# One step of a hybrid GLA/Fourier backbone: the first stage in an order by token blocks

## The reference

```python
mod = silu(cond) @ w_ada + b_ada                  # shift, scale, gate: 6 x 1024
h   = rmsnorm(x + pos, g_pre_mix) * (1 + sc_m) + sh_m
z   = h @ w_in        # [q | k | v | g | lowrank_fwd | lowrank_bwd | u]
la  = log_sigmoid(lowrank @ w_a2 + b_a2) / 16     # decays of the linear attention
o   = rmsnorm(gla(q, k, v, la, both directions), g_head) * silu(g)
y   = concat(o, real(fft2(u))) @ w_out
x   = x + gt_m * rmsnorm(y, g_post_mix)
x   = x + gt_f * rmsnorm(relu(h2 @ w_fc1)**2 @ w_fc2, g_post_mlp)
```

## Time and profile before

| | |
|---|---|
| median of three runs | 1338.31 us |
| the profiled execution's own time | 1342.97 us |
| its span, first to last instruction | 1341.2 us |
| PE busy | 1250.0 us (93%) |
| DVE, ACT, POOL busy | 774.5, 425.7, 129.7 us |
| mean granted clock of TensorE | 0.961 |
| moved by the DMA engines | 97.24 MB |

### The profile page before, as it was taken

How to read it: one execution, slowest core, us unless ns; L and a number is a source line. 1 busy time by engine, 2 the same in 40 slices (tenths; PEclk the granted TensorE clock), 3 DMA queues, 4 the chain that set the end, 5 groups by cost and what they waited for, 6 DMA issues and landing times.

```text
span 1341.2 us, 18877 instructions
## 1 busy us (share of the span) xinstructions
PE 1250.0 (93%) x7421; PEld 742.2 (55%) x7421; DVE 774.5 (58%) x1253; ACT 425.7 (32%) x736; POOL 129.7 (10%) x258
## 2 busy tenths in 40 slices
PE   2779999999896798989999999999999999999997
...
DMA packets 70894, 97.24 MB, mean 73 GB/s; under 512 B 3093, under 2 KB 53402, under 8 KB 70810
## 3 DMA queue, kind: packets, MB, share of 16 engines
...
## 4 chain that ended last, share of the span: by engine, by line
PE 55%; DVE 1%; ACT 0%; issue 0%; POOL 0%; POOLq 0%; ACTq 0%; DVEq 0%
PE bank L1221 55%; DVE region L2060 0%; DVE ghb L2060 0%; ACT bank L886 0%; ACT whi L615 0%; DVE region L2173 0%; DVE region L2175 0%; POOL small L797 0%; DVE region L2049 0%; ACT region L1137 0%; ACT region L1142 0%; DVE region L2186 0%; DVE region L2075 0%; POOL small L795 0%; POOLq L289 0%
## 5 line engine op out<-in xcount | busy, mean ns | idle before, releaser
L1221 PE MATMUL bank<-whi,region 128*128 128x512 f16 (+1 forms) x1872 | 491.4, 348 | 5.9 <-ACT region L1117 4.5
L1221 PE MATMUL bank<-region,whi 128*128 128x384 f16 (+1 forms) x1872 | 459.4, 328 | 11.0 <-DVE wlo L627 11.0
L1221 PE MATMUL bank<-wlo,region 128*128 128x512 f16 (+1 forms) x936 | 326.1, 348 | 0.0
L1221 PE MATMUL bank<-region,wlo 128*128 128x384 f16 (+1 forms) x936 | 307.3, 328 | 0.0
L1221 PEld LDWEIGHTS bank<-whi,region 128*128 128x128 f16 x1872 | 184.3, 98 | 166.2 <-issue 9.2
L1221 PEld LDWEIGHTS bank<-region,whi 128*128 128x128 f16 (+1 forms) x1872 | 183.5, 98 | 133.5 <-DVE wlo L627 11.3
L2141 DVE SCALAR_TENSOR_TENSOR region<-bank,small,region 128x512 f32<-128x512 f32 x126 | 93.2, 749 | 158.8 <-PE bank L1221 158.4
L615 ACT ACTIVATE whi<-stage,small 128x2048 f16<-128x2048 f32 (+1 forms) x42 | 82.3, 1959 | 300.6 <-PE bank L1221 294.2
L1221 PE MATMUL bank<-region 128*128 128x512 f16 (+8 forms) x802 | 160.6, 372 | 17.2 <-DVE small L1611 5.4
L2123 DVE TENSOR_TENSOR region<-region 128x384 f32<-128x384 f32 x96 | 53.5, 557 | 182.0 <-ACT region L1189 182.0
L1221 PEld LDWEIGHTS bank<-region 128*128 128x128 f16 (+4 forms) x802 | 102.0, 164 | 66.5 <-issue 13.5
...
## 6 DMA issues: line engine op xcount, KB each, us to landing
...
region<-in_x_sample SPq DMA_DIRECT2D x8, 512.0 KB, 10.8
...
```

The costliest lines, as they stand in the source:

```text
L1221: return nc.tensor.matmul(out, lhsT, rhs, start=start, stop=stop, skip_group_check=True)
```

## The change

The first stage is written out step by step for each engine.

- **Loads.** The first ada chunk comes first, then the small vectors, then tiles and chunks in turn: all ada chunks and the chunks LR and Q are loaded with x0 to x3, and x4 to x8 behind them. Six rooms hold the ada chunks in place of eight.
- **Positions.** The row half of the embedding is no longer loaded 64-fold: 16 rows are loaded, and PE multiplies them by a selection (`spread_pos`, eight f32 matmuls of 16 rows, 128 x 512). DVE copies each to `posr` (`put_pos`) and adds it (`add_pos`); the column half is added by POOL (`add_col`).
- **Blocks.** Before the gains, only x0 to x3 are turned. x4 and x5 are turned behind the first products of block 0, x6 to x8 between those of block 1. PE's order from the gains on: LR and the first Q tile of block 0, x4, x5, the second Q tile, the spread of K's maximum; LR and Q of block 1 with x6 and x7 between, K's tiles of blocks 0 and 1 with x8 between; LR and Q of block 2, the logits, K of block 2. The copies from PSUM and the high and low parts on ACT and DVE follow this order.
- **Low rank.** `low_rank_tile` puts the eight inner slices into four column groups of the array (24 matmuls with 32 columns as before, six in each group); the four partial sums stay apart on 128 partitions, and w_a2, loaded four times, adds them in the logits (128 rows in place of 32).
- **Decays.** `logits(0)` comes behind the last product of Q and behind four of K's six. From the product U_A on the order is that of before.

```diff
-    start = []
-    for what in "x0 a0 x1 a1 x2 x3 a2 x4 a3 x5 x6 a4 x7 x8 a5 a6 a7".split():
...
-    for what, n in start:
+    start = [("rows", 0), ("pos", 1), ("pos", 2), ("rows", 1), ("out", 0), ("x", 0), ("pos", 3), ("rows", 2), ("out", 1),
...
+    first = [("z", LR, 0, 0), ("z", Q, 0, 0), ("x", 4), ("x", 5), ("z", Q, 1, 0), ("sc", K),
...
-        ada_room = [R1[:, 2048 * i:2048 * i + 2048] for i in range(4)] + [R34[:, 2048 * i:2048 * i + 2048] for i in range(4)]
-        xh = [R1[:, 8192:9216], R34[:, 8192:9216]]
+        ada_room = [R1[:, 2048 * i:2048 * i + 2048] for i in range(4)] + [R34[:, 2048 * i:2048 * i + 2048] for i in range(2)]
+        xh = [R34[:, 7168:8192], R34[:, 8192:9216]]
+        lr_pair = [R34[:, 6400 + 128 * x:6528 + 128 * x].bitcast(F16) for x in range(2)]
...
+        wa2 = R34[:, 4608:4608 + 512]
+        lrS = R34[:, 5120:5120 + TOK]
+        row16 = gex[0:16].rearrange("p b n -> p (b n)")
+        row_sel = whi[1][0:16, :].bitcast(F32)
...
+            load_ada(0)
+            sp.dma_start(consts[:, 0:C_MASK], a["k_consts"][:, 0:C_MASK]).then_inc(s_const, 16)
...
-                    sp.dma_start(posr[64 * r:64 * r + 64, j - 1:j + 1],
-                                 pos_rows[r, j - 1:j + 1].partition_broadcast(64)).then_inc(s_pos[j // 2], 16)
...
+            sp.dma_start(row16, a["k_pos_row"]).then_inc(s_prow, 16)
+            sp.dma_start(posc, a["k_pos_col"]).then_inc(s_pcol, 16)
+            load_x(0)
+            load_ada(1)
...
+            sp.wait_ge(s_wa2, 1)
+            for q in range(4):
+                for d in range(2):
+                    r = 2 * RANK * q + RANK * d
+                    sp.dma_start(wa2[r:r + RANK, 256 * d:256 * d + 256], a["w_a2"][0, d]).then_inc(s_misc, 16)
...
-            for j in range(NT):
+            def add_col(j):
...
+                nc.gpsimd.tensor_tensor(x1[:, j, 512:D], x1[:, j, 512:D], posc, ALU.add).then_inc(s_posc, 1)
+            nc.gpsimd.memset(wa2, 0.0).then_inc(s_wa2, 1)
+            x_rstd(0)
+            add_col(1)
+            x_rstd(1)
+            add_col(2)
...
+            x_rstd(3)
+            add_col(4)
+            add_col(5)
+            add_col(6)
+            x_rstd(4)
+            x_rstd(5)
...
-            for what, n in start:
-                if what == "x":
-                    if n + 2 < NT:
-                        square_x(n + 2)
-                    if n + 1 < NT:
-                        norm_x(n + 1)
-                elif what == "rows":
-                    mod_part(n, ada1[n])
...
+            chunk_high(act, LR)
+            mod_part(5, ada1[5])
+            square_x(3)
+            norm_x(3)
+            mod_part(6, ada1[6])
+            chunk_high(act, Q)
+            mod_part(7, ada1[7])
             act.wait_ge(s_gn, 1)
...
+            def put_first(key):
+                _, i, m, t = key
+                bank = take_z(key)
+                dst = lrS if i == LR else (qT, kT)[i - Q][:, m, :]
+                nc.scalar.activation(dst[:, TBW * t:TBW * t + TBW], bank[:, 0:TBW], ACT.Copy,
...
+            high_x(0, 0)
+            high_x(0, 1)
+            square_x(4)
+            square_x(5)
+            norm_x(4)
+            norm_x(5)
+            put_first(("z", LR, 0, 0))
+            high_x(1, 0)
+            put_first(("z", Q, 0, 0))
...
+            chunk_high(act, K)
+            square_x(6)
+            square_x(7)
+            norm_x(6)
...
+            put_first(("z", Q, 0, 2))
+            put_first(("z", Q, 1, 2))
+            chunk_high(act, U_A)
+            decay_logs(0)
+            put_first(("z", K, 0, 2))
+            put_first(("z", K, 1, 2))
...
+            def spread_pos(j):
+                if j == 1:
+                    pe.wait_ge(s_prow, 16)
+                    pe.wait_ge(s_psel, 1)
+                bank = A.open(pe, ("pos", j))
+                mm(bank[:], row_sel[:, P * (j - 1):P * j], row16, True, True).then_inc(A.filled(("pos", j)), 1)
...
-            for i in range(G_A):
+            def low_rank_tile(key):
+                t = key[3]
+                wh, wl = pair(LR)
+                bank = A.open(pe, key)
+                toks = slice(TBW * t, TBW * t + TBW)
+                pe.wait_ge(s_tl, 2 * t + 2)
+                for kk in range(2):
+                    for n, (w, x) in enumerate(((wh, HTh), (wh, HTl), (wl, HTh))):
+                        for q in range(4):
+                            r = 2 * RANK * q
+                            ins = nc.tensor.matmul(bank[r:r + 2 * RANK, 0:TBW], w[:, 2 * q + kk, :], x[:, 2 * q + kk, toks],
+                                                   start=kk == 0 and n == 0, stop=kk == 1 and n == 2,
+                                                   tile_position=(0, r), skip_group_check=True)
+                ins.then_inc(A.filled(key), 1)
...
+                else:
+                    if step_[3] == 0 and step_[2] == 0:
+                        pe.wait_ge(s_wlo, n + 1)
+                    if n == LR:
+                        low_rank_tile(step_)
+                    else:
+                        up_tile(step_, 0, n, step_[2], step_[3], HTh, HTl).then_inc(A.filled(step_), 1)
...
-                if i == Q:
-                    logits(0)
...
             def add_pos(j):
                 dve.wait_ge(s_x[j], 16)
-                dve.wait_ge(s_pos[(j - 1) // 2], 48 if j <= 2 else 32)
-                own.did(V.tensor_tensor(x1[:, j, 0:512], x1[:, j, 0:512], posr[:, j - 1, :], ALU.add))
-                V.tensor_tensor(x1[:, j, 512:D], x1[:, j, 512:D], posc, ALU.add).then_inc(s_posd, 1)
+                A.wait_read(dve, ("pos", j))
+                V.tensor_tensor(x1[:, j, 0:512], x1[:, j, 0:512], posr[:, j - 1, :], ALU.add).then_inc(s_posd, 1)
...
+            dve.wait_ge(s_const, 16)
+            V.tensor_copy(row_sel.rearrange("p (r t) -> p r t", t=64),
+                          ident[0:16, 0:16].unsqueeze(2).to_broadcast([16, 16, 64])).then_inc(s_psel, 1)
+            def put_pos(j):
+                bank = A.take(dve, ("pos", j))
+                V.tensor_copy(posr[:, j - 1, :], bank[:]).then_inc(A.read(("pos", j)), 1)
+            put_pos(1)
...
+            mod_cols(ada1[4])
+            put_pos(7)
+            put_pos(8)
+            add_pos(3)
+            chunk_low(dve, LR)
+            chunk_max(dve, Q)
+            put_x(3)
+            set_scale(Q)
+            mod_cols(ada1[5])
+            mod_cols(ada1[6])
+            chunk_low(dve, Q)
+            mod_cols(ada1[7])
...
-            for i in range(G_A):
-                if i == LR:
-                    chunk_low(dve, 1)
-                    chunk_max(dve, 2)
-                else:
-                    chunk_max(dve, i + 2)
...
+            block_turned(dve, 0)
+            gain_x(0, 0)
+            gain_x(0, 1)
+            low_x(0, 0)
+            add_pos(4)
+            low_x(0, 1)
+            add_pos(5)
+            add_pos(6)
+            put_x(4)
+            put_x(5)
+            block_turned(dve, 1)
+            gain_x(1, 0)
+            gain_x(1, 1)
+            chunk_max(dve, K)
+            low_x(1, 0)
+            low_x(1, 1)
+            add_pos(7)
+            set_scale(K)
+            add_pos(8)
+            put_x(6)
+            chunk_low(dve, K)
+            put_x(7)
...
+            decay_bias(0)
+            chunk_max(dve, U_B)
+            chunk_low(dve, U_A)
+            set_scale(U_B)
+            decay_sums(0)
```

285 lines of the change are left out of this document (161 added, 124 removed).

## The result

The changed kernel took 1344.85 us (median of 6 runs, 1343.68 to 1348.04) beside 1338.64 for the kernel before on the same chip (6 runs, 1335.08 to 1340.33): ratio 1.0051, 95% interval 1.0037 to 1.0066. It is slower by some 6 us; the forecast was 1341, with 1330 to 1348 as its range. The profiled execution took 1344.74, with a span of 1342.9, and so lies on its median, while the profiled execution of before (1342.97) lay 4.3 over the median measured here.

A forecast was written before the change was run, and what follows sets the result against it. PE, 93% busy, was taken as the bound, with only its waits and low clock to win. Start to logits(1): 61.8 + 8.5 + 62.5 + 36.5 = 169.3 for 166.6; 1338.3 + 2.7 = 1341 us, range 1330 to 1348.

The forecast's parts named there:

- Part A: From the start to the gains being set: forecast to end at 61.8 us, 3.3 us shorter than before.
- the stretches at the full clock: In the start, three turns with a modulation row behind them bring short full-rate stretches, chance about a half each: 2 us saved.
- Wait before x3: In the start, PE stands 5 us before x3, whose positions DVE adds only behind the last two selections' copies.
- The bound that I gave for a low clock throughout: In the start, gains come at 63.8 us if PE's clock is low throughout.
- Part B: From the gains to the first product: 8.5 us for 9.8, first product at 70.3.
- Part C: From the first product to the end of logits(0): 62.5 us for 43.0, waits and clock losses included.
- Wait of block 1: Before block 1's low-rank tile, PE waits 4.5 us for the low half that DVE ends at 18.3.
- rival 3: In the low-rank tiles, column groups don't overlap, LR takes 3.9 us (7.7 at the low clock): 1350; chance 0.08.
- Part D: From the end of logits(0) to logits(1), with the serial decay chain: 36.5 us for 48.8.
- DVE's maximum: In the decay chain, V_A's maximum (2.3 us) follows both decay sums; PE waits 3.5 us behind U_A's third tile.
- The drop of the clock behind logits(0): Behind logits(0), the clock falls as before, but this costs nothing any more, since PE waits anyway.
- the base: For the whole kernel, the 2.7 us was added to the median 1338.3; the profiled execution was 4.66 over it.

## Why the prediction was right, and where it was off

**Part A, too short by 1.9 and 3.3 us.** Gains at 63.7 and 65.1 for 61.8. Three terms were too small. The first modulation row began at 9.58 and not at 8.4, since the vectors landed at 7.78, 2.5 us later than before and not 1.5. The selections at the low clock take some 1.9 each from start to start, 15.4 for all eight and not 13.6. And there is a second wait, before x2 (2.37 and 0.52). Against this stand the stretches at the full clock, put at 2 us: the one around 31 us came in one of the two profiles and saved some 2.9 us of PE time, of which the wait before x2 took more than half back (x2 began 1.2 us earlier), and the one from about 41 us on came in both and saved some 2.2. Wait before x3: 5 forecast, 5.26 found. Q's low part ahead of the last columns: 2.3 and 2.35. The bound that I gave for a low clock throughout, 63.8, was nearer than the forecast, but not because the clock was low throughout: the late start and the slower selections made up for what the full stretches gave. The sum itself has two slips: its terms end the last `mod_out` at 57.7, where the text has 57.6 for the last but one, and 57.6 + 2.3 + 3.3 + 0.3 is 63.5 and not 63.8.

That the 16-row matmuls don't hold the clock up was assumed, and the 128-row ones show it. One reading of the kernel before was wrong: the loads were said to be no bound of their own. PE waited for ACT, ACT for DVE's position adds, and DVE for what is loaded, in the view of its waits, 0 to 65 us:

```profile
DVE region L1652 <- DMA region<-in_x_sample: 17.3, 5, 8.6
```

The Trainium skill (TensorE: Matmul & The Clock Gate, Part 4: PE-mode transpose) says that the full clock doesn't engage for transposes. In the changed kernel the turn of x1 at 26.58 was followed by the full level around 31 us in one profile and not in the other, so a turn with a modulation row behind it doesn't assure it, nor does it exclude it. The two later profiles of the kernel before contradict the page as the first did: the 16 turns in a row that had taken 3.66 us took 2.25 and 2.23 there, at the full level.

**Part B** was right: 8.6 for 8.5.

**Part C, too long by 1.7 us.** Wait of block 1: 4.5 forecast, 1.15 + 3.54 found, and filling it moved logits(0) by 2.6 us with 2.28 lost elsewhere, so it was on the path. LR tile at the low clock: 1.9 forecast, 2.11 found; at the full clock 1.3 and 1.16. Behind the wait of block 1 the first Q tile took 5.78 us, as charged (5.8); in block 0 it took 4.37, a loss of 0.5 where 1.9 was charged. The five turns took 4.6 us from start to start and not 5.3. Sum 60.8 for 62.5. That the groups overlap, on which rival 3 hung, the ungrouped kernel settled: 4.08 us for 1.16, 3.5-fold. The Trainium skill (TensorE: Matmul & The Clock Gate, Part 3: Packing small matmuls — row/col tiling) has 2.38-fold for three column tiles; for four it gives no figure.

**Part D** was right: 36.8 for 36.5. DVE's maximum stood where it was forecast, and taking it out of the way gave 5.3 us. The drop of the clock behind logits(0), which the forecast took to cost nothing, didn't come at all.

That the four parts add up to 169.9 for 169.3 is in part luck: A was 1.9 us too short in the first profile and C 1.7 too long.

**The step that was mis-sized is the base.** The prediction says that the difference of 2.7 us is put "on the median", since the profiled execution took 4.66 us over it. That was to say that the excess lies outside the compared interval. More than half of it lay inside. Three profiles of before have logits(1) at 166.64, 164.57 and 161.15, 164.1 on average; two of the changed kernel have 169.93 and 171.48, 170.7. The difference is 6.6 us, and the medians differ by 6.2. Of the 3.85 us between forecast and median, some 2.5 is this base and 1.4 the parts. What lies behind logits(1) is the same within scatter: 1173.7 to 1176.8 us before, 1174.6 and 1174.8 with the change alone.

By the same averages the start gained nothing: first product at 73.0 before (74.86, 72.32, 71.91) and at 73.0 after (72.33, 73.71); the three experiments that leave the start as it is have 71.49, 72.48 and 71.32, which makes it 72.3 over five, and the spread is as wide as the difference. The waits for the loads are gone from the path, and the selections, at the low clock, took their place. The loss of 6.6 is all between the first product and logits(1). The profiles allow an estimate of what it is made of, from windows of 1 us: PE's idle time, its busy time times (1 less the granted clock), which is what the low level costs, and the rest, the work at the full clock. In us:

| first product to logits(1) | length | idle | low clock | work |
|---|---|---|---|---|
| before, three profiles | 91.8, 92.3, 89.2 | 0, 0, 0.2 | 4.2, 4.7, 1.3 | 87.6, 87.6, 87.7 |
| changed, two profiles | 97.6, 97.8 | 7.9, 7.9 | 6.2, 6.4 | 83.6, 83.5 |
| without column groups | 103.7 | 6.5 | 4.5 | 92.8 |

The work fell by 4.1: the groups save 9.2 (92.8 less 83.5), and the five turns that had stood in the start cost 4.6. The waits cost 7.8 and the low clock 2.9 more than before, which had 3.4 of it on average. Together that is the 6.6. Each kernel's work is the same to 0.2 us from profile to profile, so what makes an execution longer here is the clock: the third profile of before is shorter by some 3 us for it. So PE has less to do than before, and the two waits (4.7 and 3.2, forecast at 4.5 and 3.5) with the low clock behind them turned that into a loss.

What stays open: why one execution keeps the clock through the start and the next doesn't (47.68 and 52.89 for nearly the same code; PE waited 1.65 us before x2 in the one and 2.77 in the other), and where the other 2 us of the first profile's excess over the median lie.
